# First norm of a hybrid layer: x loaded by columns and transposed unscaled, 1/rms applied to the outputs of w_in

## The reference, cut to what matters

```python
def rmsnorm(x, g):
    xf = x.astype(jnp.float32)
    y = xf * lax.rsqrt(jnp.mean(xf * xf, axis=-1, keepdims=True) + EPS)
    return (y * g.astype(jnp.float32)).astype(x.dtype)

h = rmsnorm(x, norm_mix_g[layer])
proj = h @ w_in[layer]
dq, ckv, qi, ki, wi, mq, mk, mv, mi, mf, mo = jnp.split(proj, split_points, axis=-1)
```

## Time and profile before

| what | value |
|---|---|
| median of 3 runs | 2607.22 us (2605.32 to 2608.46) |
| the profiled execution | 2605.82 us, span 2604.1 us |
| TensorE busy | 2380.2 us (91%) |
| VectorE busy | 1533.2 us (59%) |
| ScalarE busy | 1216.1 us (47%) |
| GpSimd busy | 293.1 us (11%) |
| mean of DMA | 223 GB/s |

### The profile page before, as it was taken

How to read it: one execution, slowest core, us unless ns; L and a number is a source line. 1 busy time by engine, 2 the same in 40 slices (tenths; PEclk the granted TensorE clock), 3 DMA queues, 4 the chain that set the end, 5 groups by cost and what they waited for, 6 DMA issues and landing times.

```text
span 2604.1 us, 31395 instructions
## 1 busy us (share of the span) xinstructions
PE 2380.2 (91%) x11173; PEld 1870.8 (72%) x11173; DVE 1533.2 (59%) x1707; ACT 1216.1 (47%) x1378; POOL 293.1 (11%) x173
## 2 busy tenths in 40 slices
PE   6999999999999999999998499999999999999990
PEld 6888588667889998885887466666666666666660
DVE  4322376564335543223223588888888888888875
ACT  4222333354323432223222277777667766677751
POOL 0000000000000000000000112222222222222212
PEclk8999999999999999999999699999999999999995
DMA  4333133202434554220423489999999999999975
GB/s 174 98 96 96 48 91 96 72 25 88 148 96 146 175 182 129 97 89 1 118 97 108 159 325 410 407 400 400 407 395 403 403 401 394 398 398 406 403 318 215
DMA packets 135564, 580.28 MB, mean 223 GB/s; under 512 B 18088, under 2 KB 20304, under 8 KB 80336
## 3 DMA queue, kind: packets, MB, share of 16 engines
q1 hardware_dynamic: 130384, 562.71, 57.8%
q0 software_dynamic: 5120, 16.79, 2.0%
HBM read 571.05 MB, written 25.17 MB: 229 GB/s over the span
## 4 chain that ended last, share of the span: by engine, by line
PE 60%; DMA 18%; DVE 13%; issue 5%; ACT 4%; POOL 0%; DVEq 0%; SPq 0%; ACTq 0%; POOLq 0%
PE psd L716 42%; DMA e_raw<-in_w_gate_dram 9%; DMA e_raw<-in_w_down_dram 7%; DVE e_lo L1919 6%; PE psx L1050 2%; PE psx L1051 2%; ACT e_hi L1428 2%; PE psd L1078 2%; DVE y_sb L2042 1%; PE psd L977 1%; PE psx L1035 1%; PE psx L958 1%; ACT y_sb L1477 1%; PE psx L1058 1%; PE psx L752 1%
## 5 line engine op out<-in xcount | busy, mean ns | idle before, releaser
L1919 DVE TENSOR_TENSOR e_lo<-e_raw,e_hi 128x2048 fp32r<-128x2048 f32 x320 | 721.3, 2285 | 141.2 <-ACT e_hi L1428 139.4
L1538 DVE TENSOR_TENSOR w_lo<-w_raw,w_hi 128x1024 fp32r<-128x1024 f32 (+1 forms) x240 | 291.1, 1213 | 642.2 <-ACT w_hi L1128 642.0
L1428 ACT ACTIVATE e_hi<-e_raw 128x2048 fp32r<-128x2048 f32 x320 | 602.9, 1912 | 91.3 <-DMA e_raw<-in_w_gate_dram 69.2
L1128 ACT ACTIVATE w_hi<-w_raw 128x1024 fp32r<-128x1024 f32 (+1 forms) x240 | 252.0, 1051 | 763.7 <-PE psd L716 763.7
L1050 PE MATMUL psx<-e_hi,xt_pair 128*128 128x512 f32 x1024 | 429.5, 419 | 67.4 <-DVE e_lo L1919 61.8
L1051 PE MATMUL psx<-e_lo,xt_pair 128*128 128x512 f32 x1024 | 417.6, 408 | 0.0
L716 PE MATMUL psd<-w_hi,act_hi 128*128 128x512 f32 (+1 forms) x832 | 320.6, 385 | 6.0 <-DVE act_lo L1594 2.0
L716 PE MATMUL psd<-w_lo,act_hi 128*128 128x512 f32 (+1 forms) x832 | 319.7, 384 | 0.0
L716 PE MATMUL psd<-w_hi,act_lo 128*128 128x512 f32 (+1 forms) x832 | 319.6, 384 | 0.0
L1050 PEld LDWEIGHTS psx<-e_hi,xt_pair 128*128 128x128 f32 x1024 | 203.3, 199 | 140.7 <-DVE e_lo L1919 93.0
L651 POOL DMA_INDIRECT y_rows<-y_sb,put_idx x32 | 208.1, 6504 | 596.9 <-DVE y_sb L2042 596.9
(11 more groups left out here) (309 smaller groups left out, 2934.4 us busy)
## 6 DMA issues: line engine op xcount, KB each, us to landing
e_raw<-in_w_gate_dram SPq DMA_DIRECT2D x128, 1024.0 KB, 12.1
e_raw<-in_w_up_dram SPq DMA_DIRECT2D x128, 1024.0 KB, 7.9
e_raw<-in_w_down_dram SPq DMA_DIRECT2D x128, 1024.0 KB, 10.4
w_raw<-in_w_in_dram SPq DMA_DIRECT2D x72, 512.0 KB, 3.6
w_raw<-in_w_ckv_dram SPq DMA_DIRECT2D x64, 512.0 KB, 3.7
w_raw<-in_w_out_dram SPq DMA_DIRECT2D x32, 512.0 KB, 3.6
w_raw<-in_w_cq_dram SPq DMA_DIRECT2D x32, 512.0 KB, 3.6
w_raw<-in_w_co_dram SPq DMA_DIRECT2D x32, 512.0 KB, 3.6
```

Source lines behind the costliest of these rows:

```text
L1128: act.activation(w_hi[j % 2][:, :, 0:w], w_raw[j % 4][:, :, 0:w], ACT.Copy).then_inc(hi_done, 1)
L1428: act.activation(e_hi[n][:, :], raw_at(b, r)[:, :], ACT.Copy).then_inc(e_hi_done, 1)
L1538: dve.tensor_tensor(w_lo[j % 2][:, :, 0:w], w_raw[j % 4][:, :, 0:w], w_hi[j % 2][:, :, 0:w].bitcast(F32), ALU.subtract).then_inc(lo_done, 1)
L1919: dve.tensor_tensor(e_lo[n][:, :], raw_at(b, r)[:, :], e_hi[n][:, :].bitcast(F32), ALU.subtract).then_inc(e_lo_done, 1)
```

## The change

x is loaded in four groups of 512 columns for all tokens, each followed by one piece of w_in. The gain comes as 16 rows of 128 and is transposed by TensorE into a column per K-tile (`gain_t`). x is transposed as it is: one K-tile of all four token tiles fills one bank. ScalarE's high half and VectorE's low half multiply by the gain while they evict. Only four K-tiles are transposed before the first product; the others are transposed in pairs before pieces 1 to 6 of misc's product (`input_beside`). The squares of x run on ScalarE beside the product, the roots of all four tiles are taken at once. 1/rms (`rstd_mix`) is multiplied onto the outputs of w_in in the evictions: as a scalar per partition for misc and head_n, and for head_t, where tokens lie along the free dimension, by a row `rstd_row` that four matmuls of a matrix of ones with diagonal matrices spread over all partitions. head_t's four banks are all evicted by VectorE. Some semaphores are merged, and the small gains are loaded without a wait. The diff, cut to its core:

```diff
@@ -82,8 +82,12 @@
         misc = at("misc", [P, TT, MISC], 168)
         gain = at("gain", [P, D], 174)
         x_in = at("x_in", [P, TT, D], 96)
-        xs = [at(f"xs{r}", [P, D], 182 + 8 * r) for r in range(2)]
         junk = at("junk", [P, D], 136)
+        rstd_row = at("rstd_row", [P, T], 182)
+        gain_rows = at("gain_rows", [KT, P], 184)
+        gain_t = at("gain_t", [P, KT], 185)
+        ones_mat = at("ones_mat", [P, P], 186)
+        rstd_diag = at("rstd_diag", [P, TT, P], 188)
...
@@ -436,12 +439,12 @@
                     for j in range(4):
                         piece(NEXT[name], 0, j)
-            for t in range(TT):
-                sp.dma_start(x_in[:, t, :], x[0, t * P:(t + 1) * P, :]).then_inc(x_land[t], 16)
-                if t == 0:
-                    sp.dma_start(gain[:, :], norm_mix_g[0:1, :].to_broadcast([P, D])).then_inc(gain_land, 16)
-            for j in range(4):
-                piece("misc", 0, j, wait=False)
+            for g in range(4):
+                c = slice(512 * g, 512 * g + 512)
+                sp.dma_start(x_in[:, :, c], x[0].rearrange("(t p) d -> p t d", p=P)[:, :, c]).then_inc(x_land[g], 16)
+                if g == 0:
+                    sp.dma_start(gain_rows[:, :], norm_mix_g.rearrange("a (k p) -> (a k) p", p=P)).then_inc(gain_land, 16)
+                piece("misc", 0, g, wait=False)
...
@@ -449,24 +452,23 @@
-            sp.wait_ge(n_xs, 4)
-            sp.dma_start(kv_gain[:, :], kv_norm_g[0:1, :].to_broadcast([P, DSA_C])).then_inc(kv_land, 16)
-            sp.dma_start(ki_gain[:, :], k_idx_norm_g[0:1, :].to_broadcast([P, IDX_D])).then_inc(kv_land, 16)
+            sp.dma_start(kv_gain[:, :], kv_norm_g[0:1, :].to_broadcast([P, DSA_C])).then_inc(head_gain_land, 16)
+            sp.dma_start(ki_gain[:, :], k_idx_norm_g[0:1, :].to_broadcast([P, IDX_D])).then_inc(head_gain_land, 16)
             stream("misc")
             sp.wait_ge(bank_done[3], first["out"])
-            sp.dma_start(w_uv_s[:, :, :], w_uv[0].rearrange("(c p) h d -> p c (h d)", p=P)).then_inc(uv_land, 16)
+            sp.dma_start(w_uv_s[:, :, :], w_uv[0].rearrange("(c p) h d -> p c (h d)", p=P)).then_inc(const_land, 16)
             sp.wait_ge(pv_done, TT * DSA_H)
-            sp.dma_start(ml_gain[:, :], ml_norm_g[0:1, :].to_broadcast([P, ML_H * ML_V])).then_inc(ml_land, 16)
+            sp.dma_start(ml_gain[:, :], ml_norm_g[0:1, :].to_broadcast([P, ML_H * ML_V])).then_inc(head_gain_land, 16)
-            sp.dma_start(mem_in[:, :, :], mem[0].rearrange("(t p) d -> p t d", p=P)).then_inc(mem_land, 16)
+            sp.dma_start(mem_in[:, :, :], mem[0].rearrange("(t p) d -> p t d", p=P)).then_inc(res_land, 16)
-            sp.wait_ge(n_xs, NORM_AT["x"])
+            sp.wait_ge(n_xs, XS_AT["x"])
...
@@ -576,6 +578,7 @@
         def _(pool):
             pool.memset(ident[:, :], 0.0).then_inc(pool_own, 1)
             pool.memset(ones_col[:, :], 1.0).then_inc(consts, 1)
+            pool.memset(ones_mat[:, :], 1.0).then_inc(g_col_out, 1)
             pool.wait_ge(pool_own, 1)
             pool.affine_select(out=ident[:, :], in_=ident[:, :], compare_op=ALU.not_equal, fill=1.0, base=0,
                                pattern=[[-1, P]], channel_multiplier=1).then_inc(consts, 1)
...
@@ -752,10 +755,33 @@
                             ins = pe.transpose(psx[g][:, P * k:P * k + P], src[t % 2][:, kt * P:kt * P + P], ident[:, :])
                         ins.then_inc(n_turned, 1)
+            def turn_input(kt):
+
+                pe.wait_ge(x_land[kt // 4], 16)
+                if kt >= 4:
+                    pe.wait_ge(n_lo, kt - 3)
+                for t in range(TT):
+                    ins = pe.transpose(psx[kt % 4][:, P * t:P * t + P], x_in[:, t, kt * P:kt * P + P], ident[:, :])
+                ins.then_inc(n_turned, 1)
+
+            def input_beside(j):
+
+                if 0 < j < 7:
+                    for kt in (2 * j + 2, 2 * j + 3):
+                        turn_input(kt)
+                pe.wait_ge(n_lo, 2 * j + 2)
+
             pe.wait_ge(consts, 2)
-            turn_norm("mix", xs)
-            pe.wait_ge(n_lo, 16)
-            dense("misc", "tokens")
+            pe.wait_ge(gain_land, 16)
+            pe.transpose(psd[0][:, 0:KT], gain_rows[:, :], ident[0:KT, 0:KT]).then_inc(side_turned, 1)
+            for kt in range(4):
+                turn_input(kt)
+            pe.wait_ge(g_col_out, 2)
+            dense("misc", "tokens", beside=input_beside)
+            pe.wait_ge(rs_diag, TT)
+            for t in range(TT):
+                ins = pe.matmul(psx[0][:, P * t:P * t + P], ones_mat[:, :], rstd_diag[:, t, :], start=True, stop=True)
+            ins.then_inc(side_turned, 1)
             dense("head_t", "features")
...
@@ -1201,19 +1227,32 @@
                                    psx[g][:, :].rearrange("p (k n) -> p k n", k=4), ACT.Copy).then_inc(n_hi, 1)
                 return go
-            for t in range(TT):
-                act.wait_ge(x_land[t], 16)
-                square(x_in[:, t, :], junk[:, :], t)
-                root(t, 1)
-                if t:
-                    turned_tile("mix", t - 1, turned_to(act_hi))
+            def input_high(kt):
+                act.wait_ge(n_turned, kt + 1)
+                act.activation(act_hi[:, kt, :], psx[kt % 4][:, :], ACT.Copy, scale=gain_t[:, kt:kt + 1]).then_inc(n_hi, 1)
+
+            act.wait_ge(g_col_out, 2)
             for j in range(2):
+                for kt in (2 * j, 2 * j + 1):
+                    input_high(kt)
                 split("misc", 0, j)
-            turned_tile("mix", TT - 1, turned_to(act_hi))
-
-            dense("misc", lambda i, m: act.activation(misc[:, m, :], psd[m][:, 0:MISC], ACT.Copy))
-
-            act.wait_ge(n_xs, 4)
+
+            def input_norm(i, k):
+                if k < 6:
+                    for kt in (2 * k + 4, 2 * k + 5):
+                        input_high(kt)
+                if 2 <= k < 6:
+                    if k == 2:
+                        for g in range(4):
+                            act.wait_ge(x_land[g], 16)
+                    square(x_in[:, k - 2, :], junk[:, :], k - 2)
+                if k == 6:
+                    root(0, TT)
+                    act.wait_ge(rs_done, 1)
+
+            dense("misc", lambda i, m: act.activation(misc[:, m, :], psd[m][:, 0:MISC], ACT.Copy, scale=rstd_mix[:, m:m + 1]),
+                  beside=input_norm)
+
             for t in range(TT):
                 if t:
                     act.wait_ge(k_sq, t)
...
@@ -1224,7 +1263,7 @@
                 act.activation(relu_dot[0][:, 256:256 + IDX_D], misc[:, t, DSA_C:DSA_C + IDX_D], ACT.Square, scale=2.0,
                                accum_out=stats[:, 0, TT + t:TT + t + 1]).then_inc(k_sq, 1)
             root(0, 8)
-            dense("head_t", lambda i, m: act.activation(proj_t[:, span(i * 4 + m, 1), :], psd[m][:, :], ACT.Copy))
+            dense("head_t", None)
             act.wait_ge(k_turned, 1)
             act.activation(c_kv_t[:, 0, :], psx[0][:, :], ACT.Copy).then_inc(k_out_a, 1)
             act.wait_ge(k_turned, 3)
...
@@ -1242,7 +1281,8 @@
             def head_n_out(i, m):
-                return act.activation(proj_n[:, m, 512 * i:512 * i + 512], psd[m][:, :], ACT.Copy if i < 2 else ACT.Sigmoid)
+                return act.activation(proj_n[:, m, 512 * i:512 * i + 512], psd[m][:, :], ACT.Copy if i < 2 else ACT.Sigmoid,
+                                      scale=rstd_mix[:, m:m + 1])
...
@@ -1627,24 +1667,42 @@
             def one_of(i, m):
                 return span(i * 4 + m, 1)
-            dve.wait_ge(gain_land, 16)
-            for t in range(TT):
-                dve.wait_ge(n_sq, t + 1)
-                rstd(t, 1, 1.0 / D)
-                if t >= 2:
-                    dve.wait_ge(n_turned, 4 * (t - 1))
-                scale(x_in[:, t, :], xs, gain, t)
-                if t:
-                    turned_tile("mix", t - 1, (act_hi, act_lo))
+            def input_low(kt):
+                dve.wait_ge(n_hi, kt + 1)
+                dve.scalar_tensor_tensor(act_lo[:, kt, :], psx[kt % 4][:, :], gain_t[:, kt:kt + 1],
+                                         act_hi[:, kt, :].bitcast(F32), ALU.mult, ALU.subtract).then_inc(n_lo, 1)
+
+            dve.wait_ge(side_turned, 1)
+            dve.tensor_copy(gain_t[:, :], psd[0][:, 0:KT]).then_inc(g_col_out, 1)
             for j in range(2):
+                for kt in (2 * j, 2 * j + 1):
+                    input_low(kt)
                 split("misc", 0, j)
-            turned_tile("mix", TT - 1, (act_hi, act_lo))
-            dense("misc", lambda i, m: dve.tensor_copy(misc[:, m, :], psd[m][:, 0:MISC]))
+
+            def input_norm(i, k):
+                if k < 6:
+                    for kt in (2 * k + 4, 2 * k + 5):
+                        input_low(kt)
+                if k == 6:
+                    dve.wait_ge(n_sq, TT)
+                    rstd(0, TT, 1.0 / D)
```

(45 more changed lines are left out.)

## The result

| what | before | after |
|---|---|---|
| median of 7 runs each | 2607.22 us (2603.77 to 2612.78) | 2593.97 us (2587.08 to 2598.38) |
| ratio of the runs, 95% interval | | 0.9943 (0.9927 to 0.9959) |
| span of the profiled execution | 2604.1 us | 2585.3 us |

The change makes the kernel 13 us faster (forecast 14.7), by the interval between 11 and 19. Two more sets of timings of the same kernel gave 0.9948 (0.9936 to 0.9961) and 0.9951 (0.9938 to 0.9965).

What follows compares the result with a forecast made beforehand. The start's serial preparation before the first product was taken as the bound to change, TensorE being busy 91% overall; -24.2 + 5.6 + 2.6 + 1.7 - 0.7 + 0.3 = -14.7 gave 2592.5 us, own range 2589 to 2597, widened to 2587 to 2600.

Steps and rivals of the forecast that it cites:

- 1, the first matmul: Kernel start: scalings and most low halves leave the path, so the first matmul begins at 10.85, 24.2 us earlier.
- 2, transposes amid the product: Misc's product: eight transposes before each of six pieces cost +5.6 us, with ScalarE and VectorE work fitting beside TensorE.
- 3, the new wait: Between misc's product and head_t: waiting for 1/rms and its spreading matmuls costs +2.6 us, root's table load hidden.
- 4, the clock: TensorE's clock: falls after the new stall, +1.7 us; rises earlier at the product's start thanks to transposes, -0.7 us.
- 5, evictions: Output evictions: head_t's on VectorE alone stay hidden; the tensor scale on head_n's tails adds +0.3 us.
- B: Rival at the start: x and weight transfers come late, 5 us lost in all, 2597.5 us; chance 0.17.
- C: Rival on the clock: no fall in the stall and rise before the first matmul, 2590.1 us; chance 0.13.
- D: Rival in misc's product: transposes and short waits keep it at the lower clock throughout, +16, 2623 us; chance 0.04.
- E: Rival in later stages: time gained at the start is given back, as in the expert stage, 2607 us; chance 0.04.

Runs made afterwards that it cites:

- experiment 2: Changed kernel with a one-element Sqrt on ScalarE ahead of its first wait, so the table load runs early: 2590.64 us, ratio 0.9936.
- Experiment 6: Changed kernel with all sixteen K-tiles transposed and evicted ahead of the product instead of twelve between its pieces: 2597.66 us, ratio 0.9962.
- experiment 4: Changed kernel with 1/rms replaced by ones; root, diagonal, matmuls by ones and row copy left out, squares kept: 2597.51 us.
- experiment 7: Changed kernel with early table load, and squares, root and diagonal one piece earlier, timed twice: 2589.56 us (0.9938) and 2590.79 us (0.9928).
- experiment 1: The changed kernel again with no edit, for more timings and a second trace: 2594.95 us against 2607.24.

## Why the prediction was right

The mechanism and the sign were right: the start was the stage to change, and what was gained there was carried along. That the median lies within 1.5 us of the number given is in part luck, as the sum below shows. The steps:

**1, the first matmul (-24.2).** It came to -22.9, at 12.09 instead of 10.85. The term missing from the sum is the first table load of ScalarE. Before, it ran at 0.79 while x was on its way; now it comes when the wait for the transposes ends, and ScalarE's first high half behind it (experiment 2: 10.81). The load in the trace of before, and in that of after:

```profile
0.79 1.28 ACT L1180 ACT_TABLE_LOAD   x1 [0.79 <-PEq L2131]
...
7.75 1.28 ACT L1232 ACT_TABLE_LOAD   x1 [7.75 <-PE psx L764]
```

The prediction weighed where the root's load would stand and forgot the first one. A wait alone does not hold the load back: the square at L1180 waits too, for x, and so does the added activation of experiment 2, for `consts`, and both loads ran at 0.79. What differs in the code is that two waits stand ahead of L1232 (`g_col_out`, `n_turned`) and one ahead of the others; no run tests whether that decides it. The other links were right to 0.1 to 0.2 us: gain at 6.37 (6.25 with the landing, forecast), high half 0.70, the pair of highs 1.27; low halves with the gain took 0.7 each.

**2, transposes amid the product (+5.6).** 6 x 0.87 = 5.2, no wait of TensorE inside the product. Experiment 6 shows that the interleaving hides work rather than only moving it. The cover on ScalarE was wider than the 0.4 forecast, 0.75.

**3, the new wait (+2.6).** 2.4 by the chain: the product's last 24 matmuls began at 43.39 and end with their 3.69 at 47.08, head_t starts at 49.44; by the starts of matmuls 2.3 (behind the last one at 46.73 the next would have started at 46.88, as in experiment 4, and it did at 49.20). Idle 1.23 instead of 1.65, the diagonal 0.89 instead of 1.1, the matmuls by ones 1.16 instead of 0.9. The root's table load was hidden, as chosen. The k chain was in time, by 1.4 us: 0.1 of margin before, TensorE 2.4 later and the chain 1.2 (forecast 2.6 and 1.2).

**4, the clock (+1.7 and -0.7).** The fall after the stall did not come in any trace: the term of 1.7 was mis-sized and is 0. At the start 1.3 was saved in the first and third trace of after (first piece 3.92 against 5.2) and 0.3 lost in the second (5.48), 0.8 on average, so 0.7 was a fair mean. The rule of the Trainium skill ("TensorE: Matmul & The Clock Gate", Part 4: PE-mode transpose) that transposes don't count for the clock is not what these traces show: with 17 transposes and 1.9 us of idle time ahead, the first piece ran at 3.92, full pace, in two of three traces of one program. In the second trace it began at that pace too, and the clock fell after seven matmuls. The clock does not always rise in time: in experiment 2 and in the second trace of experiment 7 the first matmuls start 0.28 us apart.

**5, evictions (+0.3).** Nothing was added. By starts in order of time the keys' first matmul came 221.1 us after head_t's first in all three traces of after, and 221.3 in both of before.

The measured terms up to head_t: -22.9 + 5.2 + 2.3 - 1.4 (the product itself, from start to start, 29.6 instead of 31.0) = -16.8, which is the 16.8 read there. The forecast's terms up to this point, -24.2 + 5.6 + 2.6 - 0.7, make -16.7: the forgotten table load (1.3) was made up for by transposes, wait and first piece that each cost less. Behind head_t the forecast added 1.7 + 0.3, and neither came. The medians lost about 3 us all the same, for a reason that stays open, or by chance; this is where luck is in the number.

**What is open.** At k the gain is 17 us on average, and it is 16.7 at the end of the spans of the same five traces; in the medians it is 12 to 14. So on average the traced executions don't give the gain back. The traces of after fell on kinder executions: with 2587.1, 2595.9 and 2590.6 us they average 2591.2, all 18 timed ones 2593.8, while the two traces of before average 2607.9, close to the median. Most of the gap of 3 us between traces and medians is that choice. Whether the executions without a trace lost it by chance, to the granted clock, or in a stage that the change lengthens, these runs don't tell.

**Rivals.** B (late transfers) is excluded: by the gapless chain, and by ScalarE's splits, which wait for TensorE and for no transfer. (In its working 1 MB ahead of 5.64 at 393 GB/s is 3.0 us, not 2.5, and the last transfer then ends at 19.8; it changes nothing.) C (the clock kinder): both of its conditions were met in the first and third traces of after, in the second the clock had risen too, but fell again within the first piece; the medians stayed above its 2590.1. D did not happen: after the first piece the pieces take 3.69, the full pace. E did not happen on the average of the traces; of the medians 3 us stay open.

## What to carry to other kernels

A serial prologue is worth its full length, and the way out is to make the first product's operands in its own order: load by contraction columns, transpose unscaled, put a per-row factor on the outputs, and interleave the rest of the preparation with the product. When the first instruction of an engine moves behind a wait, look for the table load that may move with it; here a one-element activation ahead of the wait took it off. Leaving a function out can move a load too, as experiment 4 shows, and so blur what the experiment was to measure. A factor applied to the outputs brings a wait at the product's end: compute it a piece earlier.

## What the runs showed that was not expected

The granted clock differs between executions of one program. The first 24 matmuls took 3.92, 5.48 and 3.92 us in three traces of the changed kernel (6.12 in one of experiment 7). An idle stretch of 1.8 us ahead of the keys was followed by the lower level in both traces of before; in the first and third traces of after the same stretch was not:

```profile
268.50:270.30 1.80, 0.07 (x1) 0.00 (x0) 1.70 (x3) 0.71 (x2) 0.00 (x0) 1.00 0.00 0
270.30:276.00 5.70, 5.66 (x14) 2.58 (x15) 0.69 (x1) 0.83 (x2) 0.00 (x0) 1.00 0.33 93
```

The keys' 32 matmuls then took 13.97 instead of 15.67; in experiment 1, with the same idle stretch, 15.67 again. So the length of an idle stretch alone does not decide it. Each such fall costs some 1.7 us. Their number can well make much of the spread of 7 to 11 us between runs: over the 18 executions of the changed kernel the two shortest spans (2585.3, 2586.0) have mean clocks of 0.963 and 0.964, the three longest (2596.2 to 2597.3) 0.959 and 0.960. That is a correlation; no run sets the clock.

At the start of a trace the column of the granted clock doesn't tell the level. It reads 1.00 in experiment 2 while 17 matmuls pass in 4 us, 0.28 us apart at first, as in the first trace of after, where 26 pass:

```profile
11.00:15.00 4.00, 4.00 (x17) 4.00 (x18) 1.75 (x3) 0.57 (x1) 0.00 (x0) 1.00 1.06 387
```

There the distance between matmuls of one shape has to be read.
